# Delta rule on one core: four first taps of the values before the block substitution, the queries' normalisation directly behind it

## What is computed

```python
qkv = silu(causal_dwconv(concat([dq, dk_, dv_]), dn_conv_w))   # 4 taps per channel
cq, ck, cv = split(qkv)
cq = l2norm(cq); ck = l2norm(ck)                               # per head
...
qc = to_chunks(q) * (dk ** -0.5)
L = where(causal, exp(G[i] - G[j]), 0)
A = where(strict, einsum('bhnid,bhnjd->bhnij', k_beta, kc) * L, 0)
sol = triangular_solve(eye + A, rhs, lower=True, unit_diagonal=True)
attn = where(causal, einsum('bhnid,bhnjd->bhnij', qc, kc) * L, 0)
# then a scan over the 4 chunks with u, w (from sol), attn and the decays
```

## Time and profile before

| | |
|---|---|
| median of 3 runs | 2320.45 us (2319.55 to 2320.57) |
| profiled execution, its own time | 2317.8 us |
| its span | 2316.0 us |
| mean granted TensorE clock | 0.994 of full |
| busy: PE, DVE, ACT, POOL | 2270.0, 966.2, 860.3, 993.3 us |

### The profile page before, as it was taken

One profiled execution on the slowest core, in us unless ns is written; L12 is line 12 of the kernel. 1 busy time (PEld: TensorE's weight loads), 2 busy tenths in 40 slices (PEclk: granted clock), 3 DMA queues, 4 the chain that ended last, 5 costly groups with the idle time before them and its releaser, 6 DMA issues.

```text
span 2316.0 us, 24835 instructions
## 1 busy us (share of the span) xinstructions
PE 2270.0 (98%) x10550; PEld 1870.5 (81%) x10550; DVE 966.2 (42%) x1165; ACT 860.3 (37%) x1042; POOL 993.3 (43%) x416
## 2 busy tenths in 40 slices
PE   9999999999999999999999999998998999999997
PEld 7888778888888887888888757877878888888886
DVE  4241323441143203443234632288488233766601
ACT  4354333323322433432245364353361434322221
POOL 5437234544444651444433613444133334454542
PEclk9999999999999999999999999999999999999999
DMA  6215123322232431323233302342231233333231
GB/s 226 99 64 166 62 76 97 98 93 100 92 100 98 144 117 42 97 95 100 93 112 127 91 28 82 108 125 58 65 113 35 64 126 101 95 97 100 92 99 73
DMA packets 159998, 222.96 MB, mean 96 GB/s; under 512 B 24065, under 2 KB 85633, under 8 KB 159633
## 3 DMA queue, kind: packets, MB, share of 16 engines
q1 hardware_dynamic: 158336, 216.63, 29.4%
q10 hardware_dynamic: 1552, 4.76, 0.6%
HBM read 214.50 MB, written 6.85 MB: 96 GB/s over the span
## 4 chain that ended last, share of the span: by engine, by line
PE 86%; DVE 9%; ACT 3%; DMA 1%; issue 1%; POOL 0%; ACTq 0%; DVEq 0%
PE ps L1086 72%; PE ps L1280 2%; PE ps L1283 2%; DVE VB L2067 1%; PE ps L1296 1%; PE ps L1319 1%; DVE QN L2067 1%; PE ps L1469 1%; PE ps L1391 1%; PE ps L1404 1%; DVE KN L2067 1%; PE ps L1595 0%; DMA at_dram<-AT 0%; DVE MT L2175 0%; DVE QN L2064 0%
## 5 line engine op out<-in xcount | busy, mean ns | idle before, releaser
L559 POOL TENSOR_TENSOR w_lo<-w_raw,w_hi 128x1024 fp32r<-128x1024 f32 x378 | 951.5, 2526 | 1271.5 <-ACT w_hi L628 1271.2
L628 ACT ACTIVATE w_hi<-w_raw 128x1024 fp32r<-128x1024 f32 x378 | 395.9, 1056 | 887.9 <-DMA w_raw<-w_in 127.6
L1086 PE MATMUL ps<-XH,w_hi 128*128 128x512 f32 x1784 | 700.3, 393 | 1.5 <-ACT RLN L882 0.9
L1086 PE MATMUL ps<-XH,w_lo 128*128 128x512 f32 x1784 | 694.3, 389 | 0.0
L1086 PE MATMUL ps<-XL,w_hi 128*128 128x512 f32 x1784 | 694.0, 389 | 0.0
L1086 PE MATMUL ps<-HID,w_hi 128*128 128x512 f32 x1728 | 533.0, 390 | 0.1
L1086 PEld LDWEIGHTS ps<-XH,w_hi 128*128 128x128 f32 x1784 | 334.9, 188 | 74.3 <-issue 2.9
L1086 PEld LDWEIGHTS ps<-XL,w_hi 128*128 128x128 f32 x1784 | 335.0, 188 | 71.4 <-issue 2.9
L1086 PEld LDWEIGHTS ps<-XH,w_lo 128*128 128x128 f32 x1784 | 334.9, 188 | 70.0
L1086 PEld LDWEIGHTS ps<-HID,w_hi 128*128 128x128 f32 x1728 | 324.2, 188 | 68.4 <-issue 1.0
L1086 PE MATMUL ps<-HID,w_lo 128*128 128x512 f32 x864 | 336.2, 389 | 0.0
(11 more groups left out here) (357 smaller groups left out, 2262.9 us busy)
## 6 DMA issues: line engine op xcount, KB each, us to landing
w_raw<-w_in SPq DMA_DIRECT2D x72, 512.0 KB, 3.6
w_raw<-ffn_w_up SPq DMA_DIRECT2D x128, 256.0 KB, 2.8
w_raw<-w_up SPq DMA_DIRECT2D x88, 256.0 KB, 3.0
w_raw<-xa_wkv SPq DMA_DIRECT2D x32, 512.0 KB, 3.6
w_raw<-ffn_w_down SPq DMA_DIRECT2D x32, 512.0 KB, 3.9
w_raw<-w_in_c SPq DMA_DIRECT2D x24, 512.0 KB, 3.8
w_raw<-w_down SPq DMA_DIRECT2D x22, 512.0 KB, 3.8
w_raw<-xa_wq SPq DMA_DIRECT2D x16, 512.0 KB, 3.9
```

Of the source, the lines that this page charges most:

```text
L559: nc.gpsimd.tensor_tensor(w_lo[:, s, :, :], w_raw[:, s, :, :], w_hi[:, s, :, :].bitcast(F32), ALU.subtract).then_inc(lo_done, 1)
L628: nc.scalar.activation(w_hi[:, s, :, :], w_raw[:, s, :, :], ACT.Copy).then_inc(hi_done, 1)
L1086: mm = nc.tensor.matmul(ps[:, bank + m, :], a, b, start=start and j == 0 and n == 0, stop=stop and j == 1 and n == 2)
```

## The change

The order of three calls on DVE, in both halves of the delta rule:

```diff
@@ -2147,10 +2147,10 @@
                 evacuate(2)
+                taps(2, 0, 4)
                 block_inverses()
-                taps(2, 0, 8)
                 normalise(1, QN, LNq, float(P) ** -0.5)
-                taps(2, 8, 16)
+                taps(2, 4, 16)
                 for hh in range(4):
                     dve.wait_ge(kv_pe, 16 * q + 8 + hh + 1)
```

## The result

The changed kernel takes **2298.5 us** (median of 5 runs, 2296.85 to 2300.14) against 2320.02 us for the kernel before (5 runs, 2319.49 to 2320.57): a ratio of 0.991, 95% interval 0.9899 to 0.9921. The profiled execution took 2298.5 us for a span of 2296.7; before it was 2316.0, so the traces have 19.3 us to explain.

The account below looks back on a forecast made before the run. PE's matmuls bound the program (98% busy); gains come only where PE waits for DVE, whose path runs from substitution to ATT. Halves of -4.4 and -4.3 sum to -8.7 us from 2320.45: 2311.7 us, range 2307.5 to 2316.5.

Parts of the forecast that it names:

- (a): Four first taps ahead of the substitution: first held by w_lo until 1564.36, all done 1566.75; substitution starts 1.7 us later.
- (b): Substitution on DVE: 7.4 us of own work, stalled by two w_lo, ends at 1578.8 instead of 1574.68, 4.1 us later.
- (c): Query normalisation directly behind the substitution, 1578.8 to 1581.1; PE's 2.76 us wait at L1463 goes or nearly, worth zero alone.
- (d): DVE's later taps: expansions start at 1585.9, four taps meet them, taps end at 1593.2 instead of 1597.6, 4.4 us earlier.
- the remaining four meet expansions: 4 x 1.68: Last four DVE taps in the first half, each slowed by a GpSimd expansion to 1.68 us: 6.7 us, ending at 1593.2.
- Rival 3: DVE taps: each half's first expansion waits behind two further taps; -12.8 us in all, 2307.7 us; chance 0.08.
- The two engines take turns: DVE taps and GpSimd expansions alternate; an expansion costs 1.02 us of DVE's time, a w_lo up to 2.3.
- (e): Work behind the taps: Silu, ATT, transposes move along; split at about 1587 covered by 6 us, inverses' cover 5.7 us.
- MM's cover: Expanded inverses MM done by about 1592.7, ahead of PE's need at L1469, at 1599.0.
- (f): PE's clock: idle gap 6.5 to about 5 us, low stretch stays; no change taken, between 1.4 gained and 1.7 lost per half.

Follow-up runs that it names:

- the second: Changed kernel with the normalisation put back between the second and third four taps, so only the four first taps are moved; 2301.51 us, ratio 0.9926.
- fourth experiments: Changed kernel with the Silu of the values put ahead of the weight split on ACT; 2297.41 us, ratio 0.9906.
- the last: Changed kernel with all 16 taps behind the substitution, then the normalisation; against the kernel before only the normalisation is moved; 2342.1 us, ratio 1.0101.

## Why the prediction was wrong

Taken by its own steps, with times of the first half less 1.62 us:

- **(a), (b), (c) held.** The first tap was held by the w_lo until about 1564.6 (L2064 took 4.67 for four), the substitution was stalled by w_lo twice (2.43 and 2.28 us) and ended at 1578.6 (forecast 1578.8), the normalisation at 1580.8 (1581.1), and the wait at L1463 went. That this wait is worth nothing by itself agrees with the normalisation moved alone: the wait went, PE still started the transposes only behind ATT, and the kernel was 0.2% slower.
- **(d) failed, in the term "the remaining four meet expansions: 4 x 1.68".** The expansions were ready at 1585.1 (forecast 1585.9) and met the taps as foreseen, but not one was let in. The taps ended at 1588.7, not 1593.2: 4.5 us earlier, of which 4 x 1.02 = 4.1 is this term. Rival 3 named the direction, two more expansions kept out in each half; it was the whole rest of the stream. The prediction wrote that a stream of taps could keep the lock and put that down as rival 3, but by its own rows a kept lock is worth four expansions in each half, 2 x 4.1 = 8.2 us beyond the 8.7, or 2303.6 us (an estimate from the same rows). "The two engines take turns" was read from one stretch of the trace and taken for a property of the pair. The rule cited there, the exclusive lock of the Trainium skill (SBUF — State Buffer, "SBUF: two separate sides"), has one instruction keep the port pair while the other engine's stands. The traces agree with the blocking, in both outcomes; that an expansion stood beyond the tap that was running, through all five behind it, is what the rows show and not what that rule says.
- **(e) was right in size, wrong in what it was compared with.** The split was at 1587.7 (forecast about 1587). But its cover of 6 us was the taps, and they ended 4.5 us sooner, so that split, table load and Silu ended after ATT, and PE waited 1.56 and 0.93 us. The table load (1.28 us) is a term that the step doesn't have. The transposes began at 1592.1 instead of 1595.7: 3.6 of the 4.5 us came through. One reading in the step is wrong and changed nothing: 1.02 us is what an expansion adds to a tap, and alone it takes 1.24. MM's cover is used up too: its last expansion ended at 1595.26, and L1469 began at 1595.48, without a wait.
- **(f) failed: the clock was taken as no change.** PE's large idle gap was expected to shrink from 6.5 to about 5 us; it shrank to 1.56 and 0.93, and no low stretch came. That gave 1.5 us in the first half (L1451) and 4.7 in the second. Of the 4.7, the 1.7 in L1463 lay in slack before, so some 4.5 us came on the path, more than the 1.4 that the step allowed, which was worked out for a gap that stays.

Per half, then: forecast 4.4 and 4.3; measured in the first half 7.7 + 1.6 = 9.3, in the second 6.5 + 4.7 = 11.2. In both, the term that failed first is the same; the clock in L1451 and L1469 follows from it, since the gap ahead of them was the wait for ATT. Only the low clock in the second half's L1463 stood behind the wait for QN, which (c) took away as forecast.

## What to carry to other kernels

When VectorE and GpSimd both work on SBUF, don't price their overlap as a share: in these traces it has two outcomes, turns (1.02 us per expansion, on every tap) or exclusion for the rest of a row of taps, and one short instruction between two taps moved 11 us from one to the other. If VectorE is the path, it is worth trying to have GpSimd's work become ready within a long row of like operations, with nothing else between. That kept it out in the changed kernel and in the second and fourth experiments, and failed in the last, so it has to be looked up in the timeline each time: where it worked, the GpSimd instruction is the long one. And when a wait shrinks, recompute the covers of everything that was hidden under it, and the low clock that followed it.

## What was not expected of the hardware

**Two outcomes of the same contention.** A GpSimd tensor_tensor that becomes ready within a row of VectorE scalar_tensor_tensor operations, two operands in SBUF, either starts after the running one or stands until the row ends. The row of twelve taps kept it out for 3.6 us (4.82 less 1.24). The code's later part, which no kernel changed, shows both: eight such operations of L2243 in a row, with a w_lo beside them. In the profile of before (DVE, POOL), ready 0.52 us after the row began, it got in:

```profile
2012.34 7.52 DVE L2243 SCALAR_TENSOR_TENSOR CV<-GP,par,CV 128x512 f32<-128x512 f32 x8
...
2012.86 2.48 POOL L559 TENSOR_TENSOR w_lo<-w_raw,w_hi 128x1024 fp32r<-128x1024 f32 x1 [3.06 <-ACT w_hi L628]
```

In that of the changed kernel, ready 0.78 us after it began, it stood until the row was over, and then held the next operation (L2248, 3.31 us):

```profile
1993.06 5.38 DVE L2243 SCALAR_TENSOR_TENSOR CV<-GP,par,CV 128x512 f32<-128x512 f32 x8
1998.48 3.31 DVE L2248 TENSOR_TENSOR HF<-SA,CV 128x1024 f32<-128x1024 f32 x1
...
1993.84 6.86 POOL L559 TENSOR_TENSOR w_lo<-w_raw,w_hi 128x1024 fp32r<-128x1024 f32 x1 [3.32 <-ACT w_hi L628]
```

Such a w_lo of over 6.5 us stands there 3 times in the profile of before, 5 times in that of the changed kernel, and 6 to 9 times in those of the others, with the same instructions. Its moment of arrival bears on it: of the 100 such w_lo in the ten profiles, all 12 that were ready within 0.47 us of the row's start got in, all 45 that were ready 0.74 us or more behind it were shut out, and of the 43 between, 17 got in. For the expansions of the delta rule the outcome was the same in both halves of each kernel's profile.

**What stays open** is what decides. It isn't the kind of operation alone: in the last experiment the expansion got in between two like taps, in the second it was kept out of five. Nor was it always the first operation of a row. Nor do the row and its place decide: with all taps first, one kernel shows both. In the first half two w_lo got in between the taps of L2067; in the second half one that became ready in the sixth of them stood until the row of twelve was over (DVE of both halves, then POOL of the second):

```profile
1567.17 12.29 DVE L2067 SCALAR_TENSOR_TENSOR VB<-H,par,VB 128x511 f32<-128x511 f32 x12
...
1727.05 8.00 DVE L2067 SCALAR_TENSOR_TENSOR VB<-H,par,VB 128x511 f32<-128x511 f32 x12
...
1730.38 6.93 POOL L559 TENSOR_TENSOR w_lo<-w_raw,w_hi 128x1024 fp32r<-128x1024 f32 x1 [5.62 <-ACT w_hi L628]
```

No run varied the moment of arrival alone.

**The clock after a wait of PE.** After the waits of 4.2 us and more, at L1451 and at L1463, PE ran at half clock in part or in whole (L1451 3.47 and 3.68 us for what takes 1.91 to 1.97 otherwise). After those of up to 1.9 us it did not fall. Between them it went both ways: 2.76 us in the first half of before left L1463 at 3.84 us, 2.51 us in the second at 5.47.
